# A two-layer decoder on one NeuronCore: token projections first, norms tile by tile, square roots on ScalarE

## What is computed

```
for l in range(2):
    h = rmsnorm(x, pre_mix_g[l])
    q, k, v, u, g = split(h @ w_in[l])            # 512 columns each
    attn = dilated_mixture_attention(rotary(q), rotary(k), v)
    rec = gelu(g) * rg_lru(causal_dwconv(u))
    m = concat(rmsnorm(attn, attn_out_g[l]), rmsnorm(rec, lru_out_g[l])) @ w_out[l]
    x = x + rmsnorm(m, post_mix_g[l])
    h = rmsnorm(x, pre_ffn_g[l])
    x = x + rmsnorm(swiglu(h) if l == 0 else moe_top2_of_8(h), post_ffn_g[l])
```

## Time and profile before

| | us |
|---|---|
| median of 3 runs | 1462.04 (1459.95 to 1463.14) |
| profiled execution | 1461.06 |
| its span | 1458.7 |
| PE busy | 1437.6 (99%) |
| DVE, ACT busy | 1193.5, 1018.3 |
| POOL busy | 32.7 |

### The profile page before, as it was taken

One profiled execution on the slowest core, in us unless ns is written; L12 is line 12 of the kernel. 1 busy time (PEld: TensorE's weight loads), 2 busy tenths in 40 slices (PEclk: granted clock), 3 DMA queues, 4 the chain that ended last, 5 costly groups with the idle time before them and its releaser, 6 DMA issues.

```text
span 1458.7 us, 20727 instructions
## 1 busy us (share of the span) xinstructions
PE 1437.6 (99%) x7070; PEld 1191.9 (82%) x7070; DVE 1193.5 (82%) x1358; ACT 1018.3 (70%) x1226; POOL 32.7 (2%) x54
## 2 busy tenths in 40 slices
PE   8999999999999899999999999999999999999997
PEld 7887888888887588888888888888888888888885
DVE  7867556556676798898899889889889889989997
ACT  6665454445564587787797787788778779778774
POOL 0001000000000200000000000000000000001000
PEclk9999999999999999999999999999999999999999
DMA  9525864544433499999999999999999999999991
GB/s 364 211 100 202 343 263 184 200 193 173 174 116 130 164 385 381 367 390 384 380 383 379 379 363 400 379 360 398 384 368 389 392 366 372 402 374 367 419 399 75
DMA packets 68611, 454.11 MB, mean 311 GB/s; under 512 B 9424, under 2 KB 9552, under 8 KB 16592
## 3 DMA queue, kind: packets, MB, share of 16 engines
q1 hardware_dynamic: 60768, 432.47, 76.5%
q10 hardware_dynamic: 6640, 16.78, 3.1%
q0 software_dynamic: 1152, 4.19, 0.7%
HBM read 438.21 MB, written 15.20 MB: 311 GB/s over the span
## 4 chain that ended last, share of the span: by engine, by line
PE 95%; DVE 2%; ACT 1%; DMA 1%; POOL 0%; issue 0%; SPq 0%; DVEq 0%; ACTq 0%; POOLq 0%
PE psum L488 26%; PE psum L490 26%; PE psum L489 26%; PE psum L762 7%; PE psum L765 4%; PE psum L824 2%; ACT lru_b L940 1%; DMA ring<-in_units 1%; DVE w_lo L1191 1%; PE psum L495 1%; PE psum L646 0%; PE psum L586 0%; DVE hT_both L1202 0%; PE psum L807 0%; POOL rstd L461 0%; PE psum L524 0%
## 5 line engine op out<-in xcount | busy, mean ns | idle before, releaser
L1191 DVE TENSOR_TENSOR w_lo<-ring,w_hi 128x1024 fp32r<-128x1024 f32 x812 | 941.5, 1221 | 59.6 <-ACT w_hi L927 58.3
L927 ACT ACTIVATE w_hi<-ring 128x1024 fp32r<-128x1024 f32 x812 | 808.3, 1053 | 56.0 <-PE psum L490 50.9
L488 PE MATMUL psum<-w_hi,hT_both 128*128 128x512 f32 (+1 forms) x1088 | 424.0, 390 | 0.2 <-DVE hT_both L1202 0.2
L490 PE MATMUL psum<-w_hi,hT_both 128*128 128x512 f32 (+1 forms) x1088 | 417.6, 384 | 0.0
L489 PE MATMUL psum<-w_lo,hT_both 128*128 128x512 f32 (+1 forms) x1088 | 416.8, 383 | 0.0
L490 PEld LDWEIGHTS psum<-w_hi,hT_both 128*128 128x128 f32 x1088 | 204.4, 188 | 41.1
L488 PEld LDWEIGHTS psum<-w_hi,hT_both 128*128 128x128 f32 x1088 | 204.6, 188 | 39.6 <-issue 1.0
L489 PEld LDWEIGHTS psum<-w_lo,hT_both 128*128 128x128 f32 x1088 | 204.8, 188 | 38.1
L488 PE MATMUL psum<-w_hi,act_hi 128*128 128x512 f32 x560 | 218.7, 391 | 0.0
L490 PE MATMUL psum<-w_hi,act_lo 128*128 128x512 f32 x560 | 218.2, 390 | 0.0
L489 PE MATMUL psum<-w_lo,act_hi 128*128 128x512 f32 x560 | 218.2, 390 | 0.0
(11 more groups left out here) (233 smaller groups left out, 893.8 us busy)
## 6 DMA issues: line engine op xcount, KB each, us to landing
ring<-moe_gate SPq DMA_DIRECT2D x112, 1024.0 KB, 7.2
ring<-moe_up SPq DMA_DIRECT2D x112, 1024.0 KB, 7.5
ring<-moe_down SPq DMA_DIRECT2D x112, 1024.0 KB, 7.4
ring<-in_units SPq DMA_DIRECT2D x20, 1024.0 KB, 7.5
ring<-dense_gate SPq DMA_DIRECT2D x14, 1024.0 KB, 4.8
ring<-dense_up SPq DMA_DIRECT2D x14, 1024.0 KB, 4.9
ring<-dense_down SPq DMA_DIRECT2D x14, 1024.0 KB, 4.8
ring<-out_units SPq DMA_DIRECT2D x8, 1024.0 KB, 6.7
```

The costliest lines, as they stand in the source:

```text
L488: pe.matmul(dst, s_hi, m_hi, start=start, stop=False)
L490: return pe.matmul(dst, s_lo, m_hi, start=False, stop=stop)
L927: act.activation(w_hi[:, h % AHEAD, :], ring[:, n % RING, (h % 2) * HCOLS:(h % 2 + 1) * HCOLS], ACT.Copy).then_inc(hi_ready, 1)
L1191: dve.tensor_tensor(w_lo[:, h % AHEAD, :], ring[:, (h // 2) % RING, (h % 2) * HCOLS:(h % 2 + 1) * HCOLS], w_hi[:, h % AHEAD, :].bitcast(F3 ...
```

## The change

1. `IN_ORDER` puts the first half of q and k ahead of u and g. These two units go to banks 6 and 7, and each is used by tile: all four half units on tile 0, then the same four on tile 1; a half unit counts as done after tile 1. In layer 1 tile 1 is turned between the third and the fourth step of tile 0.
2. The rotation of that first half moves ahead of DVE's wait for the sigmoids. On ACT the splits between tanh and the root go behind the root, and those between the GeLU of the second g unit and the sigmoids go ahead of it. DVE's own splits stay ahead of its wait for the root.
3. The matmuls that sum the recurrence's squares move from ahead of the values into the fifth round of the head loop (bank 5), their small DVE steps too.
4. A norm's root is taken on ACT (`Sqrt`), and DVE takes the reciprocal (`factor`); POOL has no part in norms. `load_sqrt` is a one-column root that brings the table load ahead of the wait.
5. `norm_site` on ACT and DVE takes tile 0 through both norms, then tile 1, for the three sites where one norm follows another.
6. `last_two` computes the last two dense `down` units together, tile 0 five pieces and tile 1 three pieces last.
7. Of the four splits that DVE did between the second PRE_FFN and the router's logits one is done in the norm's site, one ahead of the first expert's low parts and two behind the pair gates.

```diff
-IN_ORDER = [6, 7, 8, 9, 0, 1, 2, 3, 4, 5]
+IN_ORDER = [0, 1, 6, 7, 8, 9, 2, 3, 4, 5]
```

On TensorE, in the mixer:

```diff
-                norm_transposes(layer, PRE_MIX)
-                channels(first, 0, layer)
-                channels(first + 1, 2)
-                channels(first + 2, 4)
-                channels(first + 3, 6)
+                norm_head(2 * layer)
+                if layer == 0:
+                    turn_rows_of(0, 1)
+                    warm(2, 4)
+                for i in range(2):
+                    norm_wait(layer, PRE_MIX, i, 0)
+                    for s in range(2):
+                        if layer > 0 and i == 1 and s == 1:
+                            turn_rows_of(2 * layer, 1)
+                        tokens(first + i, 6, i, s, (0,))
+                for i in range(2):
+                    norm_wait(layer, PRE_MIX, i, 1)
+                    for s in range(2):
+                        tokens(first + i, 6, i, s, (1,))
+                channels(first + 2, 0)
+                channels(first + 3, 2)
+                channels(first + 4, 4)
+                pe.wait_ge(qk_evac, 2 * layer + 1)
+                channels(first + 5, 6)
...
-                pe.wait_ge(gelu_ready, 2 * layer + 1)
-                for i in range(2):
-                    tokens(first + 4 + i, 4, i)
                 pe.wait_ge(gelu_ready, 2 * (layer + 1))
                 for i in range(2):
-                    tokens(first + 6 + i, 6, i)
+                    for s in range(2):
+                        tokens(first + 6 + i, 6, i, s)
...
+                    if h == 4:
+                        squares()
```

On TensorE, at the end of the dense FFN:

```diff
+            def last_two(n):
...
+                piece(1, 0, 0)
+                piece(1, 1, 0)
+                piece(1, 0, 1).then_inc(half_done, 1)
+                piece(0, 0, 0)
+                piece(0, 1, 0).then_inc(tile0_done, 1)
+                piece(1, 1, 1).then_inc(half_done, 1)
+                piece(0, 0, 1).then_inc(half_done, 1)
+                piece(0, 1, 1).then_inc(half_done, 1)
```

On ScalarE:

```diff
+                act.wait_ge(sumsq_ready, r + 1)
+                act.activation(std[:, r:r + 1], ssq[:, r:r + 1], ACT.Sqrt, scale=scale,
+                               bias=eps[:, :] if floor is None else floor).then_inc(std_ready, 1)
...
+            def norm_site(n, layer, which, tile1_halves):
...
+                load_sqrt()
+                act.wait_ge(tile0_done, n)
...
+                sumsq(stat(layer, which, 0), tokens_of(0), floor=floors[0])
+                if which == POST_MIX:
+                    keep_up(PRE_AT["in", layer, 0] + 12, AHEAD + 1)
+                sumsq_x(n, 0)
+                act.wait_ge(half_done, tile1_halves)
+                sumsq(stat(layer, which, 1), tokens_of(1), floor=floors[1])
+                norm_hi(n, 0)
+                sumsq_x(n, 1)
+                norm_hi(n, 1)
...
-                keep_up(first + 5)
                 act.wait_ge(tanh_ready, LJ * (layer + 1))
                 act.activation(lru_a[:, :, :], lru_a[:, :, :], ACT.Sqrt).then_inc(sqrt_ready, 1)
                 keep_up(first + 6)
-                act.wait_ge(rec_ready, layer + 1)
-                act.activation(lru_d[:, :, :], lru_y[:, :, :], ACT.Square).then_inc(rec2_ready, 1)
                 keep_up(first + 7)
-                keep_up(first + 8)
```

On VectorE:

```diff
+            def factor(r):
+                dve.wait_ge(std_ready, r + 1)
+                link(dve.reciprocal(rstd[:, r:r + 1], std[:, r:r + 1]))
...
+            def norm_site(n, layer, which):
+                weighted(layer, which, 0)
+                update(layer, which, 0)
+                if which == POST_MIX:
+                    keep_up(PRE_AT["in", layer, 0] + 12, AHEAD + 1)
+                normalise(n, 0)
+                weighted(layer, which, 1)
+                update(layer, which, 1)
+                norm_lo(n, 0)
+                normalise(n, 1)
+                norm_lo(n, 1)
...
-                keep_up(first + 13)
-                keep_up(first + 14)
+                if layer + 1 < LAYERS:
+                    keep_up(first + 13)
+                    keep_up(first + 14)
...
+            keep_up(NPRE - 1)
+            tok_lo(0)
...
-            tok_lo(0)
+            keep_up(NPRE)
```

More of the change, by code:

```diff
@@ L545, in channels, with tokens @@
                     mm.then_inc(half_done, 1)
[L547 to L549 removed]
+            def tokens(n, bank, i, s, tiles=range(TT)):
+                if 0 in tiles:
                     pe.wait_ge(lo_ready, 2 * n + s + 1)
[L551 to L557 removed]
@@ L559, in last_rows @@
[L559 to L570 removed]
+                w = cols(half_at(2 * n + s), 0, EC, EC)
@@ L728, in mixer, with piece @@
                         mm.then_inc(tile0_done, 1)
+            def last_two(n):
+                def piece(back, s, tt):
+                    c, h = NCH - 1 - back, 2 * (n - back) + s
+                    if tt == 0:
+                        pe.wait_ge(act_ready, c + 1)
+                        pe.wait_ge(lo_ready, h + 1)
+                    f = FPC * (c % 2) + s
+                    a = (act_hi[:, f, tt * P:(tt + 1) * P], act_lo[:, f, tt * P:(tt + 1) * P])
+                    for half in range(2):
+                        w = cols(half_at(h), half * 512, 512, D)(0)
+                        mm = product(ps[2 + 2 * tt + half], a, w, start=False, stop=(back == 0 and s == 1))
+                    return mm
+                piece(1, 0, 0)
[6 more added lines that the diff above has]
+                piece(0, 1, 1).then_inc(half_done, 1)
             def dense():
```

374 lines of the change are left out of this document (179 added, 195 removed).

## The result

| | before | after |
|---|---|---|
| median, us | 1460.99 (1459.92 to 1463.14, 4 runs) | 1474.99 (1472.47 to 1475.31, 4 runs) |
| ratio to before | | 1.0089, 95% interval 1.0077 to 1.0101 |
| profiled execution, its span | 1461.06, 1458.7 | 1475.31, 1473.5 |
| POOL busy | 32.7 | 14.5 |

The changed kernel is slower by 14.0 us (11.2 to 14.8 by the interval). The forecast was 1473; rival (b), four falls of the clock, had 1476.6.

What follows compares the result with a forecast made beforehand. TensorE, with 95% of the chain that ended last, was taken to bound the kernel. Terms 3.4 + 8.6 + 3.4 - 1.9 + 1.3 - 3.6 = +11.2 us on the median 1462.04 gave 1473; range 1464 to 1478.

Steps and rivals of the forecast that it cites:

- rival (b): All four long TensorE waits, at the start, second mixer and both turns, bring a clock fall: 1476.6 us; chance 0.17.
- The sign: Whole kernel: slower, given 0.80, against 0.10 for the same and 0.10 for faster.
- The turn of the heads (+8.6): Second half of the heads, each mixer: TensorE waits 4.3 us for VectorE's rotation, twice, +8.6 us (bounds 0 to +9.4).
- Rival (c): Not slower: rotation at the turns is in time, its chain under 21.0 us: 1461.2 us; chance 0.10.
- The start (+3.4): Program start: short first pass on tile 0 loses 3.0 us, VectorE shifts some 0.4: +3.4 us (+5.2 with a clock fall).
- The clock (+3.4): Behind the two turn waits of 4.3 us TensorE's clock falls, 1.7 us each: +3.4 us (bounds none to four falls).
- The norms (-1.9): Norm sites by tile: 0.5 us saved at each with an FFN behind, 0.9 at the dense end: -1.9 us.
- Rival (d): Faster: rotation in time, and norm sites save tile 0's whole part, some 2.5 us each: 1455.6 us; chance 0.07.
- The router (-3.6): Router: logits' copy starts 2.6 us earlier, no clock fall there, first expert's low part some 0.3 sooner: -3.6 us.
- The tail (+1.3): Roots ahead of splits at the attention's norm, 0.45 us each, and two reciprocals at the very end: +1.3 us.
- The table load: ScalarE's table loads cost 1.28 us without a drain; with the skill's 1.38 us drain, start 1.4 us later, sum 12.8.

Runs made afterwards that it cites:

- experiment 6: Changed kernel with ScalarE's two splits put back between tanh and the root, VectorE's order kept: 1472.50 us, ratio 1.0078.
- experiment 7: Changed kernel with ScalarE's and VectorE's work around the recurrence (splits, squares, rotation, masks) placed anew: 1460.74 us, ratio 1.0002.
- experiment 4: Changed kernel, but in layer 0 each of the first four half units is used on both tiles before the next: 1471.20 us, ratio 1.0073.
- experiment 5: Changed kernel with VectorE's rotary angles put behind three more splits at the start: 1473.05 us, ratio 1.0074.
- experiment 3: Changed kernel with idle matmuls, as many as fit (4, 4 and 8 at each turn), in TensorE's four long waits: 1467.81 us, ratio 1.0046.
- experiment 1: Changed kernel with VectorE's rotation and first heads' low parts ahead of the product with the root, ScalarE's squares later: 1471.69 us, ratio 1.0067.
- experiment 9: Kernel before the change with 6 idle matmuls in TensorE's wait for the router's logits: 1460.13 us, ratio 0.9991.
- experiment 10: Changed kernel with each norm step done for both tiles before the next, roots left on ScalarE: 1483.77 us, ratio 1.0152.
- experiment 8: Kernel before the change with only VectorE's router splits and the first expert's low part moved: 1456.97 us, ratio 0.9970.
- Experiment 12: Kernel of 11 with VectorE's angles behind three more splits and ScalarE's two splits around the attention's norm moved: 1453.64 us, ratio 0.9946.
- experiment 2: Changed kernel with too many idle matmuls in TensorE's four long waits (22, 22 and 36 at each turn): 1503.35 us, ratio 1.0288.
- 11: Changed kernel with the edits of experiment 4 and experiment 7 and four idle matmuls ahead of the second mixer's first product: 1456.43 us, ratio 0.9968.

## Why the prediction was right, step by step

The sign and the two waits that the largest term rests on came as forecast. But what came at the clock is rival (b), all four falls, to which I had given 0.17. The change cost 14.0 us, 14.8 between the two profiles; the forecast's sum was 11.2, that of (b) 14.6. The number itself, 1473 against 1474.99, is closer than the sum in part by luck: I added the sum to a median of 1462.04, and with a fourth run that median is 1460.99.

**The turn of the heads (+8.6)** was right in cause, place and size. VectorE and TensorE in the second mixer of the changed kernel, where G is 415.85 (answering to the earlier trace rows):

```profile
429.47 2.36 DVE L1231 TENSOR_TENSOR w_lo<-ring,w_hi 128x1024 fp32r<-128x1024 f32 x2 [3.83 <-ACT w_hi L943]
431.75 1.22 DVE L1434 TENSOR_TENSOR lru_b<-lru_b,lru_a 128x1024 f32<-128x1024 f32 x1
433.00 2.44 DVE L1436 TENSOR_TENSOR_SCAN lru_a<-lru_d,lru_b 128x256 f32<-128x256 f32 x4
435.47 1.23 DVE L1440 TENSOR_TENSOR lru_y<-lru_a,lru_g 128x1024 f32<-128x1024 f32 x1
...
440.93 0.22 DVE L1375 TENSOR_TENSOR qk<-hn 128x64 f32<-128x64 f32 x1
```

```profile
415.85 3.62 PE L577 MATMUL psum<-lru_y,blocks 128*128 128x256 f32 x16
...
441.21 1.97 PE L591 MATMUL psum<-con,qk 128*128 128x128 f32 x8 [4.19 <-DVE qk L1375]
```

and ScalarE's root:

```profile
427.36 1.06 ACT L1057 ACTIVATE lru_a<-lru_a 128x1024 f32<-128x1024 f32 x1
```

The splits end at G + 16.0 (worked out: 15.8), the recurrence at G + 20.8 (20.8), the rotation at G + 25.3 (25.3), and TensorE came at G + 21.2 (21.0). The 3.83 us ahead of the first row are VectorE standing for high parts that ScalarE makes behind the root. The root ended at 428.42, the product with it started at 431.75: 3.3 us that VectorE's two splits and their wait took. That VectorE's order holds the chain is shown by experiments 6 (1.4 us less of each wait from ScalarE's order alone) and 7 (no wait). Those two splits moved alone were not run; from these rows I estimate that 3.3 of the 4.2 us would go. Rival (c) named as its deciding point a chain under 21.0 us. Experiment 7 made one, of 20.4, by another order, and came out at 1460.74 where (c) had 1461.2; that these lie so close is partly chance, since (c) left the start at +3.4 and this kernel's start varies with its fall.

**The start (+3.4)** came as +4.8. The 3.0 us for the short first pass is in experiments 4 and 5, which gave back 4.2 and 4.1 us at the gates in two different ways; the rest is 0.3 us of shift (third half unit at 20.71 and not 20.41) and the fall behind the wait. The bound with a fall stood at 5.2.

**The clock (+3.4)** is the term that was mis-sized. I gave a fall to the two waits of 4.3 us and none to those of 2.7 and 2.9, since the nearest row was a wait of 3.1; in the profile all four had one. Rival (b), with four falls at 1.7 us, gave 1476.6; experiment 3 measured 7.2 us for the four together, 1.8 each, so the mean price was right and the count was not; single falls cost 1.5 to 2.9 by the profile. The Trainium skill, "TensorE: Matmul & The Clock Gate", HAM oscillation, says that an array which waits between bursts starts the next one throttled. This trace agrees at its four long waits, but the traces of experiments 1, 4, 6 and 7 each have a wait of 2.5 to 2.8 us with no fall behind it. At the router, whose row gave me the 1.7, the fall itself was worth only 0.9 us (experiment 9): TensorE's slower matmuls on `ones` filled time in which it would else have waited for the mask, 0.59 us, so part of the price was hidden.

**The norms (-1.9)** measured -0.5, -1.2 and -0.5, together -2.2; the wait for the low activations at the dense end is 0.89 us, 1.15 with its wake-up in the forecast. (Of the eight pieces at the dense end, four are tile 0's; one of tile 1 stands among the first five.) The reason given was half right. By experiment 10 the roots on ScalarE gave 0.7 us at a site and the order by tile about nothing where an FFN follows. Rival (d), that the order by tile saves 2.5 us at each site, has no support.

**The router (-3.6)** came as -4.0 in the profile and 4.0 alone (experiment 8), with a wait of 0.51 us for the logits. That no weight was late for the first expert was right too.

**The tail (+1.3)** came as some 1.7: the wait for the attention's low part is there, 0.67 us once in each mixer, and 0.3 us at the very end. Experiment 12 moved the splits in question, no wait for that low part is left, and each mixer is 0.9 us shorter by its profile.

**The table load.** No drain is in the trace of the changed kernel either: at its start the sum of squares ends at 6.90, the load of 1.28 us starts at 6.92, and the root at 8.21. The start did come 1.4 us over its forecast, as much as the Trainium skill's figure for the drain ("ScalarE: Activation LUTs", What ACT_TABLE_LOAD costs) would have given, but that is a coincidence: the third half unit began 0.3 us later than before, and 1.5 us are the fall behind its wait. (The sum by that figure, given as 12.8, should read 12.6.)

The terms, as the two profiles have them: 4.8 for the start with its fall, 8.4 for the two waits, 6.1 for the three other falls (1.6 behind the first turn, 2.9 behind the second, 1.6 in the second mixer), -2.2 for the norms, 1.7 for the tail, -4.0 at the router, together 14.8. The forecast of 11.2 was short by two falls that it did not count (3.1) and by the length of a third (1.2); the other terms together came out 0.7 lower than it had them.

## What to carry to other kernels

When a block of independent work is moved ahead of a dependent chain, count what is left to cover that chain, and count the other engine's queue up to it instruction by instruction: here 11 us of cover went, and two splits that stood ahead of a wait held the chain. An engine that waits for a high part while its own critical input is ready has its queue in the wrong order, and the time can be had back without giving up the move (experiment 7). Where TensorE must wait as long as here, 2.6 and 4.2 us, fill the wait with idle matmuls, counted so that they end ahead of it: that alone gave 7.2 us. Too many cost their full time (experiment 2).

## What the runs showed that I had not expected

**The length of a fall is not set by the wait ahead of it.** These are times at the lower clock, added up from windows. With the same wait of 4.2 us at the first turn it was 3.4 us in the changed kernel, 6.8 in experiments 4 and 10, and 10.2 in experiment 5; at the second turn it was 3.4 us in experiment 4 and 6.8 in the changed kernel. Every one of the eight waits of 4.2 us in the profiles of the changed kernel and of experiments 4, 5 and 10 had a fall. Those of 2.5 to 2.8 us had one sometimes: at the third half unit in two profiles of five (the changed kernel and experiment 10, not experiments 1, 6 and 7), at the start of the second mixer in the changed kernel and in experiments 1, 5 and 6, and not in 4 and 7, at one of the two turns of experiment 6, and ahead of the first normed tile in experiments 5 and 10. Where every wait at these places was under 1 us (experiments 3, 11 and 12) there was none; but one came behind the wait of 1.8 us in experiment 1, where short matmuls stood on both sides of it, and one at the start of the second mixer in experiment 10, with waits of 2.3 and 1.6 us. Why the same wait has a short, a long or no fall is open: no run here settles it.

**The spread of the times is the clock.** Kernels in which no long wait is left repeat closely: 1467.80 to 1467.94 (experiment 3), 1456.33 to 1456.67 (11), 1453.61 to 1453.78 (12). Experiment 9 is the test with one edit: one wait filled, and 3.2 us of spread became 0.6. The changed kernel, with its four falls, lay between 1472.47 and 1475.31, and experiments 4, 5 and 6 over 3.5 to 4.2 us. What goes with the spread is the long waits that are left, and not what one profile shows: the profile of experiment 7 has no fall, but its waits of 2.5 and 2.6 us are left, and its runs lie between 1459.19 with a mean clock of 0.998 and 1463.64 with 0.994. So the expected gain of an edit that leaves such waits in place can't be read from one profile: experiment 5 won 4.1 us at its place and 2 in the median.
